# Gate and up blocks with the high and the low part of x side by side in one matmul

## The reference, cut to what matters

```python
u = rms_norm_2(h, norm_pre_ffn[l])
ffn = (jax.nn.silu(u @ w_ffn_gate[l]) * (u @ w_ffn_up[l])) @ w_ffn_down[l]
h = h + rms_norm_2(ffn, norm_post_ffn[l])
```

## Time and profile before

| | |
|---|---|
| time, median of 3 runs | 4283.54 us (4274.99 to 4285.06) |
| the profiled execution | 4288.42 us, span 4287.1 us |
| TensorE busy | 3928.6 us (92%), 24004 matmuls |
| VectorE busy | 2291.8 us (53%) |
| ScalarE busy | 1784.1 us (42%) |
| chain that ended last | TensorE 78% (line 453: 66%), VectorE 11%, ScalarE 6% |
| mean granted clock of TensorE | 0.951 |

### The profile page before, as it was taken

One profiled execution on the slowest core, in us unless ns is written; L12 is line 12 of the kernel. 1 busy time (PEld: TensorE's weight loads), 2 busy tenths in 40 slices (PEclk: granted clock), 3 DMA queues, 4 the chain that ended last, 5 costly groups with the idle time before them and its releaser, 6 DMA issues.

```text
span 4287.1 us, 57523 instructions
## 1 busy us (share of the span) xinstructions
PE 3928.6 (92%) x24004; PEld 3484.0 (81%) x24004; DVE 2291.8 (53%) x3630; ACT 1784.1 (42%) x2539; POOL 106.7 (2%) x61
## 2 busy tenths in 40 slices
PE   6999988998899899778999999989898779999998
PEld 5777766877688888558999988878787569999987
DVE  4455655566555554556555544565644665454444
ACT  4444534444443443324444444444433334444443
POOL 0000000000010000000000000010000000000000
PEclk9999999999999999869999999999999689999999
DMA  5555444554354433314666666544333136666665
GB/s 183 172 153 164 127 128 122 145 162 138 114 158 128 135 112 106 99 59 143 182 183 184 183 200 194 170 123 144 105 108 94 53 108 182 183 182 186 193 194 168
DMA packets 342084, 628.88 MB, mean 147 GB/s; under 512 B 21712, under 2 KB 64672, under 8 KB 340800
## 3 DMA queue, kind: packets, MB, share of 16 engines
q1 hardware_dynamic: 330888, 609.46, 47.8%
q10 hardware_dynamic: 10936, 15.75, 1.2%
HBM read 623.04 MB, written 2.10 MB: 146 GB/s over the span
## 4 chain that ended last, share of the span: by engine, by line
PE 78%; DVE 11%; ACT 6%; issue 2%; POOL 2%; ACTq 1%; DMA 0%; DVEq 0%; POOLq 0%
PE bank L453 66%; DVE weights_low L377 3%; ACT weights_high L375 2%; DVE arena L914 1%; PE bank L1076 1%; PE bank L1171 1%; PE bank L2191 1%; PE bank L2178 1%; PE bank L575 1%; PE bank L2190 1%; POOL stat L536 1%; DVE arena L1819 1%; PE bank L1079 1%; POOL arena L1786 1%; PE bank L1155 1%
## 5 line engine op out<-in xcount | busy, mean ns | idle before, releaser
L377 DVE TENSOR_TENSOR weights_low<-weights,weights_high 128x1024 fp32r<-128x1024 f32 (+4 forms) x1176 | 1399.2, 1193 | 1432.0 <-ACT weights_high L375 1425.3
L375 ACT ACTIVATE weights_high<-weights 128x1024 fp32r<-128x1024 f32 (+4 forms) x1176 | 1207.6, 1029 | 1275.7 <-PE bank L453 1246.6
L453 PE MATMUL bank<-x_high,weights_high 128*128 128x256 f32 x3776 | 1082.7, 287 | 28.2 <-DVE weights_low L377 12.3
L453 PE MATMUL bank<-x_low,weights_high 128*128 128x256 f32 x3776 | 1076.3, 285 | 0.0
L453 PE MATMUL bank<-x_high,weights_low 128*128 128x256 f32 x3776 | 1075.8, 285 | 0.0
L453 PEld LDWEIGHTS bank<-x_high,weights_high 128*128 128x128 f32 x3776 | 732.7, 194 | 38.1 <-DVE weights_low L377 25.0
L453 PEld LDWEIGHTS bank<-x_low,weights_high 128*128 128x128 f32 x3776 | 732.9, 194 | 0.0
L453 PEld LDWEIGHTS bank<-x_high,weights_low 128*128 128x128 f32 x3776 | 732.7, 194 | 0.0
L453 PE MATMUL bank<-weights_high,x_high 128*128 128x512 f32 (+3 forms) x1408 | 572.1, 406 | 69.2 <-DVE x_low L580 34.1
L453 PE MATMUL bank<-weights_high,x_low 128*128 128x512 f32 (+3 forms) x1408 | 547.1, 389 | 0.0
L453 PE MATMUL bank<-weights_low,x_high 128*128 128x512 f32 (+3 forms) x1408 | 546.7, 388 | 0.0
(11 more groups left out here) (377 smaller groups left out, 3677.4 us busy)
## 6 DMA issues: line engine op xcount, KB each, us to landing
weights<-in_w_in_dram SPq DMA_DIRECT2D x208, 512.0 KB, 3.7
weights<-in_w_ffn_gate_dram SPq DMA_DIRECT2D x176, 512.0 KB, 4.3
weights<-in_w_ffn_up_dram SPq DMA_DIRECT2D x176, 512.0 KB, 4.2
weights<-in_w_ffn_down_dram SPq DMA_DIRECT2D x176, 512.0 KB, 4.8
weights<-in_w_out_dram SPq DMA_DIRECT2D x128, 512.0 KB, 3.8
weights<-in_even_w_in_dram SPq DMA_DIRECT2D x88, 512.0 KB, 3.6
weights<-in_odd_w_in_dram SPq DMA_DIRECT2D x80, 512.0 KB, 3.7
weights<-in_mem_w_kv_dram SPq DMA_DIRECT2D x32, 512.0 KB, 4.4
```

Of the source, the lines that this page charges most:

```text
L375: dve.wait_ge(self.high_split.count(nc.scalar.activation(high, raw, ACT.Copy)))
L377: nc.vector.tensor_tensor(low, raw, high.bitcast(F32), ALU.subtract))
L453: ins = nc.tensor.matmul(out, l, r, start=(u == 0 and c == 0 and x + y == 0), stop=(u == blk.n - 1 and c == UNIT - 1 and y == 1))
```

## The change

The high and the low part of x become one tensor `x_parts`, with `x_high` and `x_low` as its two halves at the same places as before. Gate and up blocks become a new kind, "joined". For each bank and each group of 128 rows a joined block issues two matmuls in place of three: w_high against both parts of x, 2 x 256 = 512 columns that fill the whole bank, and w_low against x_high, 256 columns onto the bank's left half. So the left half gathers x_high w_high + x_high w_low and the right half x_low w_high. In the evacuation VectorE first adds the halves with a `tensor_reduce` over pairs that lie 256 columns apart, waits for it, and then does the multiplication as before, now from SBUF. The bank is given back after the reduce. Other "features" blocks and the "tokens" blocks stay as they are.

```diff
-            xh = sb("x_high", [P, KC, S], F32R)
-            xl = sb("x_low", [P, KC, S], F32R)
+            x_parts = sb("x_parts", [P, 2, KC, S], F32R)
+            xh, xl = x_parts[:, 0, :, :], x_parts[:, 1, :, :]
...
-            self.in_X = lambda: Stationary(xh, xl, [None] * KC)
+            self.in_X = lambda: Stationary(xh, xl, [None] * KC, x_parts)
...
+                first, last = u == 0 and c == 0, u == blk.n - 1 and c == UNIT - 1
+                if blk.kind == "joined":
+                    cut = slice(n * P, (n + 1) * P)
+                    nc.tensor.matmul(self.ps[b][:, :].rearrange("p (x s) -> p x s", x=2), high[:, c, cut], blk.AT.both[:, :, k, :],
+                                     start=first, stop=False)
+                    ins = nc.tensor.matmul(self.ps[b][:, 0:S], low[:, c, cut], blk.AT.high[:, k, :], start=False, stop=last)
+                    continue
...
-            self.features(n + f"gate{i}", L.hT2, A["w_ffn_gate_2"][l], i * TILE, 4, self.gate_out(L), 0)
-            self.features(n + f"up{i}", L.hT2, A["w_ffn_up_2"][l], i * TILE, 4, self.up_out(L, i), 4)
+            self.features(n + f"gate{i}", L.hT2, A["w_ffn_gate_2"][l], i * TILE, 4, self.gate_out(L), 0, kind="joined")
+            self.features(n + f"up{i}", L.hT2, A["w_ffn_up_2"][l], i * TILE, 4, self.up_out(L, i), 4, kind="joined")
...
             dve.wait_ge(mark, L.ffn.row_mark)
-            m = dve.did(nc.vector.tensor_tensor(gate[:, j, :], self.ps[b][:, 0:S], L.ffn.row, ALU.mult))
+            m = dve.seq(nc.vector.tensor_reduce(gate[:, j, :], self.ps[b][:, :].rearrange("p (x s) -> p s x", x=2), AX.X, ALU.add))
             self.bank_free[b] = [m]
+            m = dve.did(nc.vector.tensor_tensor(gate[:, j, :], gate[:, j, :], L.ffn.row, ALU.mult))
             act.wait_ge(m)
...
             dve.wait_ge(mark, L.silu[j])
-            m = dve.did(nc.vector.tensor_tensor(prod[:, j, :], gate[:, j, :], self.ps[b][:, 0:S], ALU.mult))
+            m = dve.seq(nc.vector.tensor_reduce(prod[:, j, :], self.ps[b][:, :].rearrange("p (x s) -> p s x", x=2), AX.X, ALU.add))
             self.bank_free[b] = [m]
+            m = dve.did(nc.vector.tensor_tensor(prod[:, j, :], prod[:, j, :], gate[:, j, :], ALU.mult))
```

More of the change, by code:

```diff
@@ L166 @@
     ready: list
+    both: object = None
     pieces: dict = field(default_factory=dict)
@@ L343, in tokens, with features @@
                        AT, row0 // P, need))
-    def features(self, name, AT, W, col, chunks, evac, bank0=0, need=None):
+    def features(self, name, AT, W, col, chunks, evac, bank0=0, need=None, kind="features"):
         self.pair = 0
-        self.add(Block(name, "features", self.by_unit(W, 0, D, col, chunks * P), D // (UNIT * P), chunks * P,
+        self.add(Block(name, kind, self.by_unit(W, 0, D, col, chunks * P), D // (UNIT * P), chunks * P,
                        tuple(range(bank0, bank0 + chunks)), evac, AT, 0, need))
@@ L446, in matmul_unit @@
                 pe.wait_ge(*blk.AT.ready[k])
+                first, last = u == 0 and c == 0, u == blk.n - 1 and c == UNIT - 1
[5 more added lines that the diff above has]
+                    continue
                 for x, y in ((0, 0), (1, 0), (0, 1)):
                     wt, xt = (high, low)[y], (blk.AT.high, blk.AT.low)[x]
-                    if blk.kind == "tokens":
-                        out, l, r = self.ps[b][:, 0:w], xt[:, k, n * P:(n + 1) * P], wt[:, c, 0:w]
-                    else:
+                    if blk.kind == "features":
                         out, l, r = self.ps[b][:, 0:S], wt[:, c, n * P:(n + 1) * P], xt[:, k, :]
-                    ins = nc.tensor.matmul(out, l, r, start=(u == 0 and c == 0 and x + y == 0),
-                                           stop=(u == blk.n - 1 and c == UNIT - 1 and y == 1))
+                        ins = nc.tensor.matmul(out, l, r, start=(first and x + y == 0), stop=(last and y == 1))
+                        continue
+                    ins = nc.tensor.matmul(self.ps[b][:, 0:w], xt[:, k, n * P:(n + 1) * P], wt[:, c, 0:w],
+                                           start=(first and x + y == 0), stop=(last and y == 1))
             if u == blk.n - 1 and n < len(blk.banks) - 1:
```

## The result

The changed kernel takes 4334.49 us (median of 4 runs, 4331.81 to 4337.23), the kernel before 4283.24 beside it. The ratio is 1.0123, 95% interval 1.0106 to 1.0141: slower by 51 us, and forecast was 4336. The profiled execution took 4333.7 us with a span of 4332.4.

A forecast was written before the change was run, and what follows sets the result against it. TensorE, busy 92% of the span, was taken as the bound. From the profiled 4288.4 us, -37.5 saving, +79.2 delays, +11 clock and -4.9 to the runs' median gave 4336 us; range 4290 to 4370 for 8 in 10.

The forecast's parts named there:

- TensorE's saving: Gate and up blocks: 2816 groups of three matmuls become two, 0.360 to 0.3467 us each, saving 37.5 us.
- chain of a bank, d: VectorE at a block's end, per bank: reduce 0.685, wait 0.04, multiply 0.355, together 1.08 us.
- delay after gate: TensorE waits for the low weights of unit g+3 after each of 22 gate blocks, 1.32 us.
- delay after up: TensorE waits for the low weights of unit g+3 after each of 20 up blocks, 2.20 us.
- at a layer's end, added: After each layer's last up block, TensorE's existing 0.7 us wait grows by 3.1 us, twice.
- all delays: TensorE's waits after 22 gate blocks, 20 up blocks and two layers' ends, summed to 79.2 us.
- half speed in these blocks: TensorE's clock: a third of 22 pauses after up blocks and both long ones lose 1.2 us each, 11 us.
- 0.2267 + 0.120, which two rows give: One 512-column step plus one 256-column step on TensorE make a group of 0.3467 us, from profile rows.
- bound of 0.360: TensorE saves nothing, a group staying at 0.360 us, if the halves 16 KB apart stream like two matmuls.
- rival 1: Evacuation: the reduce costs like its 256 outputs, 0.415 us, so the time is 4278 us; chance 0.12.
- Rival 3: Evacuation: the reduce is slower through a 1 KB stride inside the bank; at 0.85 us, 4365 us; chance 0.06.
- my 13 ns a matmul: TensorE: a fixed 13 to 14 ns comes with each matmul beyond its columns, seen at three widths.

## Why the prediction was right, point by point

The forecast was 4336 us and the time is 4334. The mechanism held at each place that it named. That the figures meet to 2 us is luck: the changed part lost 7 us more than the sum says, and the rest of the program, which the change doesn't touch, ran shorter beside it.

| term | forecast | measured |
|---|---|---|
| TensorE's saving | 37.5 us | 150 x (2.880 - 2.773) + 202 x (2.880 - 2.827) = 26.8 |
| chain of a bank, d | 1.08 us | 1.06 |
| delay after gate | 1.32 us | 1.15 or 1.31, by the pace before it; 22 make 27.9 |
| delay after up | 2.20 us | 2.05 or 2.21; 20 make 41.8 |
| at a layer's end, added | 3.1 us | 3.6 - 0.7 = 2.9 |
| all delays | 79.2 us | 27.9 + 41.8 + 5.8 = 75.5 |
| half speed in these blocks | 11 us | 7 stretches x 1.5 = 10.5 |
| sum | +52.7 us | +59.2 |

A delay is here the idle time that the profile shows, 0.16 us by which the narrow matmul's record outlasts its step, and the 0.10 us that the first matmul takes longer. The two layers' stretches grew by 1566.1 - 1506.4 = 59.7 us, against the 59.2 of the terms.

- **TensorE's saving was mis-sized**, by 11 us of 37.5. The step that failed is "0.2267 + 0.120, which two rows give": 0.3467 us a pair is right for 150 of the 352 units, and in the other 202 a pair takes 0.353. Both rows stand for streams of one width, and the stream of 256 columns has one pace in the kernel before, 2.88 us in every unit. The bound of 0.360 was on the right side. The halves' distance, which I had named as the reason for that bound, has nothing to do with it; the kernel with adjacent halves shows so.
- **The chain** was right to 2%. The reduce over pairs out of a bank, which no row of before showed, takes 0.683 us for 512 inputs, like the rows; rival 1 would have needed 0.45.
- **The delays** at the pace of the forecast are those of the forecast, 1.31 and 2.21 us against 1.32 and 2.20. Behind a span at the slower pace they are smaller by what the longer unit gives, 3 x 0.053 = 0.16 us more room. This is why the wrong saving did little harm. A shorter unit raises the delays: per us of unit 352 us are saved and 44 x 3 = 132 come back.
- **The clock**: 5 stretches of 3.4 us at half speed behind the 20 pauses after up blocks, and one at each layer's end; I had taken a third of 22 and both ends. A stretch loses 1.5 us rather than 1.2. The first of them in the changed kernel, by stretch and in TensorE's timeline, and the one at the first layer's end:

```profile
2073.20:2076.60 3.40, 3.40 (x13) 2.92 (x12) 0.72 (x1) 0.53 (x1) 0.00 (x0) 0.50 0.95 345
```

```profile
2073.22 0.63 PE L451 MATMUL bank<-x_parts,weights_high 128*128 128x512 f32 x1
...
2075.78 0.63 PE L451 MATMUL bank<-x_parts,weights_high 128*128 128x512 f32 x1
```

```profile
2512.67 0.50 PE L461 MATMUL bank<-weights_high,ff_high 128*128 128x512 f32 x1 [3.62 <-DVE weights_low L378]
...
2513.86 0.63 PE L461 MATMUL bank<-weights_high,ff_low 128*128 128x512 f32 x1
```

  In the first, four pairs take 2.56 us, 0.64 each, so 3.4 us hold 5.3 pairs in place of 9.6, and 4.3 x 0.353 = 1.5 us are lost.

- **What the sum leaves.** The stretches grew by 59.7 us, but the profiled spans differ by only 4332.4 - 4287.1 = 45.3 and the medians by 51. So the rest of the program took 14 us less in the changed kernel's trace: 3 us ahead of the first gate block, 9 between the layers, and 2 behind the last down block. Outside the stretches that trace has 393 us at half speed and the kernel before's 415; 22 x 0.45 = 10 us, with the ratio of pair times above as a stand-in for those matmuls. The change edits nothing there. In the ten traces of this case the part between the layers takes from 790 to 801 us, and the part ahead of the first gate block, which runs before anything that was changed, from 1962 to 1969. Why it varies stays open.
- **Rival 3**, a slow stride inside the bank, is out as well: 0.683 us.

The Trainium skill's rule of 2.5 ns for each matmul (TensorE: Matmul & The Clock Gate, Back-to-back issue gap), which that section gives for isolated matmuls, would give a saving of 7 us. The joined matmuls alone, which show no pauses at the blocks' ends, saved 0.053 us a unit, 0.0067 a pair, so 352 x 0.053 = 18.7 us. That rule was not met; my 13 ns a matmul was met in the spans at 0.347 us a pair, and half of it in the others.

## What to carry to other kernels

Before a change that makes an evacuation longer, look at what is queued behind it on the same engine, and add up the time until the bottleneck engine needs that: here four chains of 1.06 us stood ahead of a split that had 1.2 to 2 us to spare. An engine that is half idle on average can still be the bound at the end of each block, and the remedy is the order of its queue: with the split issued first the same work ran in 4256 us in place of 4334, and with the matmuls two by two in 4242, 0.9% under the kernel before. Step times read from streams of equal matmuls gave the pace of a mixed stream in 150 of its 352 units and were 2% short in the others, so such a sum needs a range.

## What the runs showed of the hardware that I had not expected

- Matmuls of 512 and 256 columns that alternate singly take 0.347 or 0.353 us a pair, at full granted clock in both cases. In the changed kernel the pace is taken anew at a pause or a change of clock, 19 of 42 spans at the first and 23 at the second; in the two kernels without such pauses (the joined matmuls alone, and the split first) it is 0.353 throughout. Two by two it is 0.348, eight by eight 0.349; streams of their own would give 0.2267 + 0.120 = 0.347. At the slower pace the 256-column step is 0.117 and the 512-column step 0.236.
- 512 moving columns from two places 16 KB apart run as fast as 512 in one run.
- Pauses of 1.8 to 1.95 us after up blocks were followed by half speed 5 times in 20 in the changed kernel and 6 in 20 with adjacent halves, pauses of 0.9 to 1.1 us after gate blocks never, the 20 pauses of 1.6 us in the kernel with the evacuation alone never either, and those of 2.7 us and more in the kernel with the longer chain 40 times in 44.
- The traces show 379 to 415 us at half speed outside the two layers' stretches, though the work there is the same in all kernels. By the ratio above some 15 us of time go with that, which no edit asked for.
